# Exponentials left unscaled and the scale put on the result, in two attentions, and a heads stage that begins with keys and values

## The chip, the cores and the metric

One core of a Trainium2 chip runs the whole program in one launch. The metric is device microseconds (us) from start to end. A core has five engines, each with an instruction stream of its own: PE (matrix multiplies; a matmul's stationary operand is loaded by a weight load, shown as PEld), DVE (vector), ACT (scalar functions), POOL (GpSimd) and SP, which here only issues DMAs. They wait for each other through semaphores. PSUM has 8 banks of 128 x 512 fp32; PE writes them, DVE and ACT empty them.

## The reference

The program is one inference step of a small encoder trunk for two groups of frames: 1024 new frames of one stream (the prompt, 8 tiles of 128 rows) and 64 frames of another that has 512 cached ones (the sample, a ninth tile of 64 rows). In transposed form there are T = 1088 columns, cut into chunks of 384, 384 and 320.

The even layer has two head groups from one input projection (an mLSTM, and a latent attention, MLA, 8 heads of 64 with a low-rank latent for keys and values and one for queries), one output projection over both, and a feed-forward. The odd layer has a chunk-band attention (16 heads of 64, a window of about 640 keys with a bias) and a feed-forward. Cut to the part that the change touches:

```
cq = rmsnorm(h @ W_dq, g_q)            # query latent, 384 wide
q_nope, q_rope = cq @ W_uq ...         # per head 64 + 32
k_nope, v      = ckv @ W_uk, ckv @ W_uv
p = softmax(scale * q.k + mask)        # MLA, causal by chunk of 64 frames
o = p @ v                              # o: (frames, 64) per head
x = x + concat(o_mlstm, o_mla) @ W_out
...
p = softmax(q.k + bias)                # band attention
o = p @ v
x = x + concat(o) @ W_o
```

## The kernel before

Most matmuls take fp32 data split in two parts, high and low (names in hi and lo), and make three passes (hi.hi, lo.hi, hi.lo) at the fast rate; ACT rounds the high part, DVE or POOL subtracts for the low one. Transposes and the product of probabilities with V stay plain fp32, in which one matmul shows as two records. The stages run one after the other, with a barrier between: load, mix0 (input projection and mLSTM), heads (queries, keys and values per head, from the latents, parked in HBM), mix0b (MLA attention and output projection), a feed-forward, mix (band attention with all its projections), a feed-forward and the final norm.

**Heads.** Items are one PSUM bank each: 8 tiles of weights for queries by 3 chunks (L1403), 4 tiles of key weights by 4 spans of 400 keys, then 13 tiles for values. Three results wait ahead of it: the norm of the query latent cqT, made at the end of mix0 (matmuls with ones L528, DVE L849 and L852, ACT root L775, DVE product L857), its high part (ACT L1415) and its low part (DVE L1447).

**mix0b.** Heads go in pairs; a pair has 18 steps, 9 query tiles for head e = 0 in the order S (sample), 0 to 7, and 9 for e = 1 in the order S, 7 to 0: 72 steps g in all. PE's order in a step is written by hand:

- turn(g), transposes of the probabilities p (L1672), which wait for DVE's `normal`;
- score(g+1), the scores into pS (L1662);
- fillers, 2 or 3 groups of the output projection (L1637 to L1639), each into one of three banks F in rotation;
- weigh(g) (L1691), after ACT has copied the transposed p out as pT (keep, L1744 to L1748) and after the step before has emptied pO.

ACT's order is keep(g), exp(g+1) (L1734, which also sums each row), splits, and high(g) (L1754), the high part of pO. DVE's is maximum(g+1) (L1801), one emptied filler bank (L1794), normalise(g+1) (reciprocal L1809, then p times it, L1811), the other fillers, and low(g) (L1817). p has a single buffer. The output projection of a pair's own heads begins when all 18 steps have been split. SP loads queries, keys, values and weights by the step; `splits` is a table of the steps in which a unit of output weights is loaded.

**mix.** The same shape for 8 pairs of heads, 144 steps, tiles in the order 0 to 3, S, 4 to 7 for both e: turn L2194, score L2183, fillers from a list by step (projections for the next pair L2129 to L2131, output projection of the pair before L2141 to L2143, transposes L2151 and L2161), weigh L2212. DVE: L2393 adds the bias and takes the minimum, L2403 and L2405 normalise, L2364 adds the output groups to xT, L2413 is low. ACT: keep L2282, exp L2272, high L2293. In the last three steps of pairs 1 to 6 there are 6, 6 and 6 output groups, behind a block of transposes in the last, with three banks F for them. The first pair has no output groups beside it; the last has one or two in most steps and none of the projections.

## Time and profile before

| what | value |
|---|---|
| time, median of 3 runs | 3272.31 us (3272.21 to 3276.55) |
| the profiled execution | 3272.54 us, of which 3270.5 are the span |
| PE, share of the span | 93%, weight loads 90% |
| DVE, ACT, POOL | 38%, 31%, 26% |
| heads | 417 to 502 us |
| mix0b | 502 to 864 us |
| mix (band attention) | 1680 to 2427 us |

Read it so: PE works nearly all the time, so a change can gain only where PE waits, or by fewer or cheaper matmuls. In mix0b PE is busy for 300 of 362 us, in mix for 697 of 747, so there is some waiting in both, and there is more at the seams of the stages.

### The profile page before, as it was taken

The page shows a single profiled execution, that of the slowest core. Times are in us where ns is not written, and L with a number is a line of the kernel's source. Part 1 is how long each engine was busy: PE and PEld are TensorE (multiplying, and loading weights), DVE is VectorE, ACT ScalarE, POOL GpSimd, SP SyncE. Part 2 cuts the span into 40 slices and gives each one's busy share as a digit, 9 for nine tenths or more (in the row PEclk, how much of TensorE's full clock was granted, in tenths as well). Part 3 has the DMA queues.
Part 4 walks back from the last instruction along what each step waited for, and adds up shares of the span by engine and source line. Part 5 has one row for each costly group of instructions (what it writes and reads, how often), then busy time and mean ns, then how long its engine had stood idle before and what let it go on. Part 6 is the DMA issues. An engine that isn't in the chain of part 4 may idle for free. (4 is left out here: it accounts for less than half of the span.)

```text
span 3270.5 us, 46685 instructions
## 1 busy us (share of the span) xinstructions
PE 3056.0 (93%) x18884; PEld 2956.9 (90%) x18884; DVE 1257.3 (38%) x2672; ACT 1015.3 (31%) x1772; POOL 862.5 (26%) x437
## 2 busy tenths in 40 slices
PE   6999986888899999999989999999879999999998
PEld 5889976778799999999979899999859999999997
DVE  4423335666622222222243556666653222222223
ACT  4322234444421112121134544444443111121211
POOL 3211122211332223222233322323324222232220
PEclk8999988899999999999999999999999999999999
DMA  3133133111211111111021111111111111112101
GB/s 114 56 73 65 42 143 102 47 44 34 65 52 39 38 38 40 63 38 51 0 69 43 44 37 43 39 41 44 34 48 56 52 38 38 38 38 64 38 13 61
DMA packets 153853, 165.72 MB, mean 51 GB/s; under 512 B 9063, under 2 KB 137015, under 8 KB 153535
## 3 DMA queue, kind: packets, MB, share of 16 engines
q1 hardware_dynamic: 153726, 163.96, 16.4%
q8 instruction: 89, 1.46, 0.2%
q14 instruction: 38, 0.30, 0.0%
HBM read 140.78 MB, written 28.92 MB: 52 GB/s over the span
## 5 line engine op out<-in xcount | busy, mean ns | idle before, releaser
L236 PE MATMUL ffn_banks<-hhi,ffn_whi 128*128 128x384 f32 (+1 forms) x2112 | 693.0, 328 | 19.5 <-POOL hlo L217 13.2
L237 PE MATMUL ffn_banks<-hlo,ffn_whi 128*128 128x384 f32 (+1 forms) x2112 | 692.5, 328 | 0.0
L238 PE MATMUL ffn_banks<-hhi,ffn_wlo 128*128 128x384 f32 (+1 forms) x2112 | 692.3, 328 | 0.0
L1211 DVE TENSOR_TENSOR ffn_act<-ffn_silu,ffn_banks 128x384 f32<-128x384 f32 x132 | 70.2, 532 | 962.3 <-PE ffn_banks L238 945.7
L236 PEld LDWEIGHTS ffn_banks<-hhi,ffn_whi 128*128 128x128 f32 x2112 | 399.5, 189 | 21.0 <-issue 21.0
L1145 POOL TENSOR_TENSOR ffn_wlo<-ffn_stage,ffn_whi 128x2048 fp32r<-128x2048 f32 x66 | 303.3, 4609 | 423.7 <-ACT ffn_whi L1105 423.7
L237 PEld LDWEIGHTS ffn_banks<-hlo,ffn_whi 128*128 128x128 f32 x2112 | 399.3, 189 | 0.0
L238 PEld LDWEIGHTS ffn_banks<-hhi,ffn_wlo 128*128 128x128 f32 x2112 | 399.2, 189 | 0.0
L1217 DVE TENSOR_TENSOR xT<-xT,ffn_banks 128x384 f32<-128x384 f32 (+1 forms) x528 | 281.0, 532 | 240.4 <-PE ffn_banks L238 240.4
L238 PE MATMUL ffn_banks<-ffn_ahi,ffn_wlo 128*128 128x384 f32 (+1 forms) x1056 | 344.7, 326 | 0.0
L237 PE MATMUL ffn_banks<-ffn_alo,ffn_whi 128*128 128x384 f32 (+1 forms) x1056 | 344.6, 326 | 0.0
L236 PE MATMUL ffn_banks<-ffn_ahi,ffn_whi 128*128 128x384 f32 (+1 forms) x1056 | 344.6, 326 | 0.0
L1152 POOL TENSOR_TENSOR ffn_alo<-ffn_act,ffn_ahi 128x384 fp32r<-128x384 f32 x132 | 128.0, 970 | 792.7 <-ACT ffn_ahi L1117 792.7
L1113 ACT ACTIVATE ffn_silu<-ffn_banks 128x384 f32<-128x384 f32 x132 | 62.4, 474 | 620.5 <-PE ffn_banks L238 620.5
L1105 ACT ACTIVATE ffn_whi<-ffn_stage 128x2048 fp32r<-128x2048 f32 x66 | 124.1, 1909 | 363.6 <-PE ffn_banks L238 358.5
L2129 PE MATMUL mix_F<-hhi,mix_whi 128*128 128x384 f32 (+1 forms) x576 | 194.1, 337 | 7.9 <-POOL hlo L217 7.6
L238 PEld LDWEIGHTS ffn_banks<-ffn_ahi,ffn_wlo 128*128 128x128 f32 x1056 | 198.3, 188 | 0.0
L236 PEld LDWEIGHTS ffn_banks<-ffn_ahi,ffn_whi 128*128 128x128 f32 x1056 | 198.3, 188 | 0.0
L237 PEld LDWEIGHTS ffn_banks<-ffn_alo,ffn_whi 128*128 128x128 f32 x1056 | 198.3, 188 | 0.0
L2131 PE MATMUL mix_F<-hhi,mix_wlo 128*128 128x384 f32 (+1 forms) x576 | 189.7, 329 | 0.0
L2130 PE MATMUL mix_F<-hlo,mix_whi 128*128 128x384 f32 (+1 forms) x576 | 189.4, 329 | 0.0
L482 PE MATMUL mix_F<-hhi,mix_whi 128*128 128x384 f32 (+1 forms) x528 | 180.0, 341 | 7.7 <-POOL hlo L217 7.6
(323 smaller groups left out, 5580.9 us busy)
## 6 DMA issues: line engine op xcount, KB each, us to landing
ffn_stage<-in_w_gate SPq DMA_DIRECT2D x22, 1024.0 KB
ffn_stage<-in_w_up SPq DMA_DIRECT2D x22, 1024.0 KB, 5.3
ffn_stage<-in_w_down SPq DMA_DIRECT2D x22, 1024.0 KB, 4.9
mix_wst<-in_w_qkv SPq DMA_DIRECT2D x24, 512.0 KB
mix_wst<-in_w_in SPq DMA_DIRECT2D x22, 512.0 KB
load_xin<-in_x_prompt SPq DMA_DIRECT2D x8, 512.0 KB, 4.6
mix0b_wst<-in_w_out SPq DMA_DIRECT2D x8, 512.0 KB
mix_wst<-in_w_out SPq DMA_DIRECT2D x8, 512.0 KB
```

What stands on the lines that cost most here:

```text
L236: nc.tensor.matmul(out, whi[:, k, :], hhi[:, k, c0:c0 + w], start=(k == 0), stop=False)
L237: nc.tensor.matmul(out, whi[:, k, :], hlo[:, k, c0:c0 + w], start=False, stop=False)
L238: last = nc.tensor.matmul(out, wlo[:, k, :], hhi[:, k, c0:c0 + w], start=False, stop=(k == kts - 1))
L482: nc.tensor.matmul(dst, wh, hhi[:, k, c0:c0 + w], start=(k == 0), stop=False)
L1105: nc.scalar.activation(whi[m][:], stage[m][:], ACT.Copy).then_inc(w_hi[m], 1)
L1145: nc.gpsimd.tensor_tensor(wlo[m][:], stage[m][:], whi[m][:], ALU.subtract).then_inc(w_lo[m], 1)
L1152: nc.gpsimd.tensor_tensor(alo[:, f, c0:c0 + w], act32[:, f, 0:w], ahi[:, f, c0:c0 + w], ALU.subtract).then_inc(a_lo, 1)
L1211: nc.vector.tensor_tensor(act32[:, f, 0:w], silu[:, f, 0:w], banks[:, 2 * f + 1, 0:w], ALU.mult).then_inc(product, 1)
L1217: nc.vector.tensor_tensor(x, x, banks[:, 4 + k % 4, 0:w], ALU.add).then_inc(added, 1)
L2129: nc.tensor.matmul(dst[:, 0:w], wh, hhi[:, k, c0:c0 + w], start=(k == 0), stop=False)
L2130: nc.tensor.matmul(dst[:, 0:w], wh, hlo[:, k, c0:c0 + w], start=False, stop=False)
L2131: last = nc.tensor.matmul(dst[:, 0:w], wl, hhi[:, k, c0:c0 + w], start=False, stop=(k == KT - 1))
```

## The change

1. **Scale moved behind the product.** In both attentions p is no longer multiplied by the reciprocal of its row sum. turn(g) waits for the exponentials alone. Since the scale belongs to a query row, the product is turned round: weigh now loads pT as the stationary operand and moves the 64 columns of V of its own head, so pO is query rows by 64. DVE's evict(g) multiplies pO by the reciprocal into a new buffer otok (query rows by the pair's 128 columns).
2. **Flips.** The output projection wants the result transposed and split. High and low per step (two operations for each of 216 steps) go; in their place stands one flip for each pair and tile (36 in mix0b, 72 in mix): a PE transpose of otok into a bank of F, ACT's high part from the bank, DVE's low part, which frees the bank. A flip is the first item of work in each of the pair's steps 10 to 17 and in the next pair's step 0. ACT takes it after exp(g+1); DVE, which empties banks in order, takes it before the step's other banks.
3. **DVE order.** maximum or minimum (g+1), reciprocal(g), all the banks of step g, evict(g).
4. **mix0b's start and SP.** Keys are loaded and split ahead of the queries, the first low part of the keys is DVE's rather than POOL's, the rotary parts have semaphores of their own, and in each step the load of output weights comes ahead of those of queries and keys.
5. **Heads.** The norm of the query latent moves from mix0's end into heads. Items are now 4 key tiles (a matmul of the norm behind each of the first three), 13 value tiles, and the query tiles last. The norm and its splits are placed among the value items. The latent of keys and values is split in 4 spans. Values have 6 output slots, each bank a semaphore pair.

```diff
@@ both attentions: turn, weigh, DVE @@
-                pe.wait_ge(s["normal"], g + 1)
+                pe.wait_ge(s["exped"], g + 1)
...
                 if g:
-                    pe.wait_ge(s["lo"], g)
+                    pe.wait_ge(s["evicted"], g)
                 for b, (_, kw, vt) in enumerate(tiles):
-                    last = nc.tensor.matmul(pO[:, 0:w], V[0:kw, vt, :], pT[0:kw, b * P:b * P + w],
+                    last = nc.tensor.matmul(pO[0:w, 0:H], pT[0:kw, b * P:b * P + w], V[0:kw, vt, own(e)],
                                             start=(b == 0), stop=(b == len(tiles) - 1))
...
-                v.tensor_scalar(p_[0:w, 0:width], p_[0:w, 0:width], inv[0:w, col], None, ALU.mult).then_inc(s["normal"], 1)
+            def evict(g):
...
+                dve.wait_ge(s["summed"], g + 1)
+                v.tensor_scalar(otok[0:w, t, own(e)], pO[0:w, 0:H], inv[0:w, g % 4:g % 4 + 1], None, ALU.mult)\
+                 .then_inc(s["evicted"], 1)
@@ mix0b: the order of work @@
+    def flips(g):
+        if g == 0:
+            return []
+        pair, n = divmod(g - 1, STEPS)
+        return [("flip", pair, ORDER[1][n - N])] if n >= N else []
+
+    def work(g):
+        return flips(g) + fillers(g)
...
+                if x[0] == "flip":
+                    _, pair, t = x
+                    w = tile_width(t)
+                    pe.wait_ge(s["evicted"], STEPS * pair + N + ORDER[1].index(t) + 1)
+                    if n >= FB:
+                        pe.wait_ge(emptied[n % FB], n // FB)
+                    nc.tensor.transpose(F[:, n % FB, 0:w], otok[0:w, t, :], S["ident"][0:w, 0:w]).then_inc(filled[n % FB], 1)
+                    return
...
                 keep(g)
                 if g + 1 < PAIRS * STEPS:
                     exp(g + 1)
+                for x in flips(g):
+                    high(x)
...
-                high(g)
...
             for g in range(PAIRS * STEPS):
                 pair, n = divmod(g, STEPS)
                 h, i = divmod(g, N)
+                if g in splits:
+                    load_w(splits[g])
                 if i == 2 and h + 2 < B_HEADS:
                     load_q(h + 2)
                 if i == 4 and h + 2 < B_HEADS:
                     load_k(h + 2)
-                if g in splits:
-                    load_w(splits[g])
@@ mix: the list of work by step @@
+        if s > N:
+            x.append(("flip", p, TILES[s - N - 1]))
+        if s == 0 and p:
+            x.append(("flip", p - 1, TILES[-1]))
@@ mix, DVE @@
             for g in range(PAIRS * STEPS):
-                work = fillers(g // STEPS, g % STEPS)
-                early = 0 if any(x[0] == "proj" for x in work) else len(work) // 2
                 if g + 1 < PAIRS * STEPS:
                     minimum(g + 1)
-                for x in work[:early]:
+                reciprocal(g)
+                for x in fillers(g // STEPS, g % STEPS):
                     empty(x)
-                if g + 1 < PAIRS * STEPS:
-                    normalise(g + 1)
-                for x in work[early:]:
-                    empty(x)
-                low(g)
+                evict(g)
@@ end of mix0 @@
-            for c in range(NC):
-                mean_of("cq_mean", c, cq_var, Q_RANK)
-            normalise(cqT, RQ, G_Q, cq_var, 2)
@@ heads @@
+    for i in range(4):
+        items += [("k", i, n) for n in range(len(spans))]
+        if i < NC:
+            items.append(("cq", i))
+    items += [("v", n) for n in range(VN)]
...
+                    if n == 2:
+                        dve.wait_ge(s["rooted"], 1)
+                        for k in range(RQ):
+                            dve.scalar_tensor_tensor(out=cqT[:, k, :], in0=cqT[:, k, :], scalar=S["gains"][:, G_Q + k:G_Q + k + 1],
+                                                     in1=var[:], op0=ALU.mult, op1=ALU.mult).then_inc(s["normed"], 1)
+                    if n == 8:
+                        dve.wait_ge(s["q_hi"], 1)
+                        dve.tensor_tensor(q_lo, cqT[:], q_hi, ALU.subtract).then_inc(s["q_lo"], 1)
```

First, DVE in mix (mix_pS are the scores, mix_F the ring of banks, mix_pO the product of the attention): one of a pair's last steps, with six output groups. Before:

```order
L2393 ISA mix_p,mix_least<-mix_pS,mix_nb 128x640
L2393 ISA mix_least 128x1
L2364 TENSOR_TENSOR xT<-xT,mix_F 128x384 x3
L2403 RECIPROCAL mix_inv<-mix_total 128x1
L2405 TENSOR_SCALAR mix_p<-mix_p,mix_inv 128x640
L2364 TENSOR_TENSOR xT<-xT,mix_F 128x384 x3
L2413 TENSOR_TENSOR mix_o_lo<-mix_pO,mix_o_hi 64x128
```

And now, the same step:

```order
L2525 ISA mix_p,mix_least<-mix_pS,mix_nb 128x640
L2525 ISA mix_least 128x1
L2535 RECIPROCAL mix_inv<-mix_total 128x1
L2473 TENSOR_TENSOR mix_o_lo<-mix_F,mix_o_hi 128x128
L2496 TENSOR_TENSOR xT<-xT,mix_F 128x384 x6
L2542 TENSOR_SCALAR mix_otok<-mix_pO,mix_inv 128x64
```

The product over 640 columns is gone, and the low part (L2473), which waits for ACT, now stands ahead of all six banks instead of behind them.

Second, PE in the same stage, from the scores of one step to its weigh. Before:

```order
L2183 MATMUL mix_pS<-mix_kk,mix_qb 128x384
L2141 MATMUL mix_F<-mix_o_hi,mix_whi 128x384
L2142 MATMUL mix_F<-mix_o_lo,mix_whi 128x384
L2143 MATMUL mix_F<-mix_o_hi,mix_wlo 128x384
L2141 MATMUL mix_F<-mix_o_hi,mix_whi 128x384
...
L2212 MATMUL mix_pO<-mix_pT,mix_V 128x128 x5
```

And now:

```order
L2310 MATMUL mix_pS<-mix_kk,mix_qb 128x384
L2270 MATMUL mix_F<-ident,mix_otok 128x128
L2263 MATMUL mix_F<-mix_o_hi,mix_whi 128x384
L2264 MATMUL mix_F<-mix_o_lo,mix_whi 128x384
L2265 MATMUL mix_F<-mix_o_hi,mix_wlo 128x384
...
L2339 MATMUL mix_pO<-mix_V,mix_pT 128x64 x5
```

One transpose (L2270) has come in ahead of the output groups and takes one of the three banks of F; weigh has as many matmuls as before, with 64 moving columns.

Third, SP in mix0b, about step 12, where mix0b_wst is the buffer of output weights, mix0b_q_in and mix0b_k_in those of queries and keys. Before:

```order
L1583 DMA mix0b_V<-park_heads_v 128x4x128
L1585 DMA mix0b_V<-park_heads_v 64x128
L1562 DMA mix0b_q_in<-park_heads_q 64x1088
L1564 DMA mix0b_q_in<-park_heads_q 32x1088
L1557 DMA mix0b_wst<-in_w_out 128x1024
L1569 DMA mix0b_k_in<-park_heads_k 64x1600
```

And now:

```order
L1686 DMA mix0b_V<-park_heads_v 128x4x128
L1688 DMA mix0b_V<-park_heads_v 64x128
L1660 DMA mix0b_wst<-in_w_out 128x1024
L1665 DMA mix0b_q_in<-park_heads_q 64x1088
L1667 DMA mix0b_q_in<-park_heads_q 32x1088
L1672 DMA mix0b_k_in<-park_heads_k 64x1600
```

The load of the weights has moved past the two loads of queries, which wait for their buffer.

## Rows read from the trace of the kernel before

**Rows 1.** The page's line of engines: busy us, share, instructions.

```profile
PE 3056.0 (93%) x18884; PEld 2956.9 (90%) x18884; DVE 1257.3 (38%) x2672; ACT 1015.3 (31%) x1772; POOL 862.5 (26%) x437
```

**Rows 2.** Timeline, end of mix0 and start of heads.

```profile
402.91 3.71 PE L528 MATMUL mix_F<-mix_raw,ones 128*128 128x384 f32 x12
...
411.89 3.88 DVE L857 SCALAR_TENSOR_TENSOR latents_cqT<-latents_cqT,gains,mix_kw 128x1088 f32<-128x1088 f32 x3 [1.18 <-ACT mix_kw L775]
...
416.87 2.92 ACT L1415 ACTIVATE hhi<-latents_cqT 128x3264 fp32r<-128x3264 f32 x1 [5.01 <-PEq L64]
...
419.82 3.56 DVE L1447 TENSOR_TENSOR hlo<-latents_cqT,hhi 128x3264 fp32r<-128x3264 f32 x1 [4.05 <-ACT hhi L1415]
...
424.38 0.66 PE L1403 MATMUL heads_bank<-hhi,heads_w_hi 128*128 128x384 f32 x1 [17.76 <-POOL heads_w_lo L1437]
```

**Rows 3.** Tile heads_w_in: users, min, median and max ns, and DMA landing.

```profile
L1413 ACT ACTIVATE heads_w_hi<-heads_w_in x12: 409/517/526, 419.7 to 471.7; 128x384 fp32r<-128x384 f32 x8, 128x256 fp32r<-128x256 f32 x4
L1437 POOL TENSOR_TENSOR heads_w_lo<-heads_w_in,heads_w_hi x12: 740/1010/4250, 420.3 to 472.2; 128x384 fp32r<-128x384 f32 x8, 128x256 fp32r<-128x256 f32 x4
DMA to landing us min/median/max: 2.4/2.7/3.1
```

**Rows 4.** Timeline, end of heads: the last park, and mix0b's first DMA.

```profile
499.77 0.32 SPq L1377 DMA_DIRECT2D park_heads_v<-heads_out  x1
502.68 0.48 SPq L1562 DMA_DIRECT2D mix0b_q_in<-park_heads_q  x1
```

**Rows 5.** Stretches of time in mix0; the granted clock follows POOL's column.

```profile
205.50:211.30 5.80, 0.15 (x1) 0.16 (x2) 5.56 (x4) 2.32 (x4) 3.04 (x1) 0.66 0.40 116
211.30:216.00 4.70, 4.70 (x19) 4.25 (x20) 1.69 (x3) 0.34 (x2) 0.00 (x0) 0.50 0.12 33
```

**Rows 6.** Groups by shape, PE in mix0b: busy, mean ns, idle before and releaser.

```profile
L1691 PE MATMUL mix0b_pO<-mix0b_pT,mix0b_V 128*128 128x128 f32 x576 | 77.8, 282 | 12.8 <-ACT mix0b_pT L1744 10.8 <-DVE hlo L1817 2.0
L1672 PE MATMUL mix0b_pP<-ident,mix0b_p 128*128 128x128 f32 x288 | 46.5, 290 | 28.1 <-DVE mix0b_p L1811 27.1
L1672 PE MATMUL mix0b_pP<-ident,mix0b_p 64*128 64x64 f32 x32 | 3.9, 246 | 4.8 <-DVE mix0b_p L1811 4.8
```

**Rows 7.** Timeline of mix0b: weighs at 564, 587 and 594 us.

```profile
564.27 1.36 PE L1691 MATMUL mix0b_pO<-mix0b_pT,mix0b_V 128*128 128x64 f32 x10
...
585.12 1.06 ACT L1715 ACTIVATE mix0b_whi<-mix0b_wst 128x1024 fp32r<-128x1024 f32 x1 [8.44 <-DMA mix0b_wst<-in_w_out]
...
587.36 2.93 PE L1691 MATMUL mix0b_pO<-mix0b_pT,mix0b_V 128*128 128x128 f32 x12 [6.63 <-ACT mix0b_pT L1744]
...
593.91 1.28 PE L1691 MATMUL mix0b_pO<-mix0b_pT,mix0b_V 128*128 128x128 f32 x10
...
594.47 0.49 DVE L1811 TENSOR_SCALAR mix0b_p<-mix0b_p,mix0b_inv 128x512 f32<-128x512 f32 x1
...
595.02 0.66 PE L1672 MATMUL mix0b_pP<-ident,mix0b_p 128*128 128x128 f32 x4
```

**Rows 8.** Groups by shape, PE in the whole of mix, columns as in rows 6.

```profile
L2194 PE MATMUL mix_pP<-ident,mix_p 128*128 128x128 f32 x480 | 76.3, 279 | 28.3 <-DVE mix_p L2405 28.3
```

**Rows 9.** The same for pairs 1 to 6, then for the last pair.

```profile
L2194 PE MATMUL mix_pP<-ident,mix_p 128*128 128x128 f32 x365 | 57.5, 278 | 11.5 <-DVE mix_p L2405 11.5
L2194 PE MATMUL mix_pP<-ident,mix_p 128*128 128x128 f32 x60 | 9.9, 285 | 13.8 <-DVE mix_p L2405 13.8
```

**Rows 10.** Timeline of one of a pair's last steps in mix.

```profile
2156.32 0.34 PE L2141 MATMUL mix_F<-mix_o_hi,mix_whi 128*128 128x384 f32 x1
...
2156.52 0.82 DVE L2393 CUSTOM_DVE_ANT_0 mix_p<-mix_pS,mix_nb 128x640 f32<-128x640 f32 x1 [0.53 <-PE mix_pS L2183]
...
2157.27 1.48 DVE L2364 TENSOR_TENSOR xT<-xT,mix_F 128x384 f32<-128x384 f32 x3
2157.36 0.33 PE L2141 MATMUL mix_F<-mix_o_hi,mix_whi 128*128 128x384 f32 x1
2157.39 0.83 ACT L2272 ACTIVATE mix_p<-mix_p,mix_least 128x640 f32<-128x640 f32 x1 [0.75 <-DVE mix_least L2393]
```

More of the change, by code:

```diff
@@ L520, in mean @@
                 return last
-            def cq_mean(x):
-                c = x[1]
-                c0, w = CHUNKS[c]
-                dst = begin(x)[:, 0:w]
-                pe.wait_ge(s["sq"], NC + RQ - 1 + c + 1)
-                for k in range(RQ):
-                    last = nc.tensor.matmul(dst, S["ones"][:], raw[:, k, c0:c0 + w], start=(k == 0), stop=(k == RQ - 1))
-                return last
             def cached(x):
@@ L1375, in _ @@
[L1375 to L1379 removed]
+            for i in range(4):
+                load(i + 2)
+                park_k(i)
+                if i == NC - 1:
+                    await_filled(sp, ("cq", NC - 1))
+                    sp.dma_start(rope[:], D["rope_q"]).then_inc(s["rope_in"], 16)
@@ L1416, in _, with square @@
+            def square(c):
+                c0, w = CHUNKS[c]
+                if c:
+                    await_filled(act, ("cq", c - 1))
+                act.activation(sq[:, :, 0:w], cqT[:, :, c0:c0 + w], ACT.Square).then_inc(s["sq"], 1)
+            high(0)
             split_w(0)
+            for n in range(1, len(spans)):
+                high(n)
+            square(0)
             split_w(1)
-            act.activation(kv_hi[:], ckvT[:], ACT.Copy).then_inc(s["hi"], 1)
-            act.wait_ge(s["v_loaded"], 16)
@@ L1432, in _ @@
         @block.gpsimd
         def _(pool):
-            for i in range(len(tiles)):
-                kts = RQ if tiles[i][2] == "q" else RK
+            for i, (name, _) in enumerate(tiles):
+                kts = RK if name == "w_uk" else RQ
                 pool.wait_ge(s["w_hi"], i + 1)
@@ L1475, in mix0b_stage @@
+                    dve.tensor_tensor(dst, dst, turned[:, c0:c0 + w], ALU.add).then_inc(emptied[number[x] % FB], 1)
 def mix0b_stage(nc, S, D):
@@ L1498, in mix0b_stage @@
     FB = 3
-    number = {x: n for n, x in enumerate(groups)}
+    def flips(g):
[5 more added lines that the diff above has]
+        return flips(g) + fillers(g)
+    END = PAIRS * STEPS
+    program = [x for g in range(END) for x in work(g)] + flips(END) + behind
+    number = {x: n for n, x in enumerate(program)}
+    flip_no = {x: n for n, x in enumerate(x for x in program if x[0] == "flip")}
     def begun(g):
@@ L1700, in _ @@
                     score(g + 1)
-                for x in fillers(g):
+                for x in work(g):
                     fill(x)
                 weigh(g)
-            for x in behind:
+            for x in flips(END) + behind:
                 fill(x)
@@ L1778, in _ @@
                     split_w(splits[g])
-                high(g)
+            for x in flips(END):
+                high(x)
         @block.vector
@@ L1845, in _ @@
                     split_q(h + 1)
-                low(g)
-            for x in behind:
+                evict(g)
+            for x in flips(END) + behind:
                 empty(x)
@@ L1947, in mix1_stage @@
     ahead += [("kc", 0, 0), ("vtok", 0, 0)]
-    behind = [("out", PAIRS - 1, j, c) for j, c in outs]
+    behind = [("flip", PAIRS - 1, TILES[-1])] + [("out", PAIRS - 1, j, c) for j, c in outs]
     def key_of(x):
@@ L2143, in fill @@
                     last = nc.tensor.matmul(dst[:, 0:w], wl, oh, start=False, stop=True)
+                elif kind == "flip":
+                    _, pair, t = x
+                    w = tile_width(t)
+                    pe.wait_ge(s["evicted"], STEPS * pair + N + TILES.index(t) + 1)
+                    last = nc.tensor.transpose(dst[:, 0:w], otok[0:w, t, :], S["ident"][0:w, 0:w])
                 elif kind == "vtok":
@@ L2258, in take @@
                     nc.scalar.activation(kk[own(e), e, T:KEYS], bank(x)[own(e), :], ACT.Copy).then_inc(s["kc_hi"], 1)
+                elif x[0] == "flip":
+                    _, pair, t = x
+                    w = tile_width(t)
+                    await_filled(act, x)
+                    nc.scalar.activation(o_hi[:, pair % 2, t * P:t * P + w], bank(x)[:, 0:w], ACT.Copy).then_inc(s["hi"], 1)
                 elif x[0] == "ktok":
@@ L2333, in _ @@
                     split_w(unit_no[weights_at(pair, n)])
-                high(g)
+            take(behind[0])
         @block.vector
```

429 lines of the change are left out of this document (248 added, 181 removed).

## The prediction

> **What bounds the kernel now.** I read the page's line of engines first: PE is busy for 93% of the span [rows 1], so only PE's waits, or fewer or cheaper matmuls, can pay. Next came the groups by shape in the two attention stages, for what ended PE's waits. In mix0b the transposes of p waited 28.1 and 4.8 us for DVE's product with the reciprocal, and weigh waited 12.8 us [rows 6]; in mix the transposes waited 28.3 us for the same product [rows 8]. Last I read the timelines at the places where these waits are long, and at the seam before heads, where PE stands for 17.76 us [rows 2]. A wait is worth its length only if nothing else is late behind it, so each is followed to what is late next.
>
> **Heads: -11.2 us.** Before, the last chunk of the query latent's norm begins on PE at 402.91, the product L857 ends at 415.77, a barrier follows to 416.85, ACT's high part takes 2.92 and DVE's low part 3.56, and the first matmul starts at 424.38 [rows 2]. Now none of it stands ahead of the first item. mix0's own PE work ends without the norm matmuls: they were last from 402.9 on, and a first group of six (1.9 us, half of the 3.71 for twelve) stood further ahead, so it ends at about 401. I add 0.7 for the last evictions, 1.1 for the barrier (from 415.77 to 416.85), 2.7 for the load of the weights, 0.4 and 0.74 for their high and low parts (smallest values of [rows 3]): PE starts at 406.6, 17.8 us earlier. The norm's matmuls come into heads: 1.9 + 3.7 = 5.6 us [rows 2]. The clock gives nothing back: after 5.8 us of idle PE the granted clock was still 0.50 for the next 4.7 us in mix0 [rows 5], as it is after a long wait, and the new pause is as long (401 to 406.6).
>
> What is late next is the low part of the query latent. DVE cannot empty value banks until the last key park has landed, by my estimate 5 us into the values (a load of 128 KB took 2.7 [rows 3], and the last park, with the barrier, 2.9 [rows 4]; a key park is several times as large). Then it has nine copies of .65 (.49 for 384 columns [rows 10], scaled to 512), 3.88 for the norm and 3.56 for the low part [rows 2]: 5 + 5.9 + 3.9 + 3.6 = 18.4 us. PE has 13 value items of six matmuls of .23 (.173 for 384 columns [rows 10]): 18.0. With the handovers that is a stall of about 1 us. Sum: -17.8 + 5.6 + 1 = -11.2. Bounds: -15 (no stall, and the pause short enough that the clock stays up for a part) and -3 (DVE's chain 8 us late, since DVE and POOL pass each other badly here: POOL's part of the weights took 4.25 us in its longest case, with DVE at work beside it, against 1.01 [rows 3]).
>
> The start of mix0b has the keys ahead of the queries, but the first exponential waits on ACT behind the split of the first block of mLSTM output, the last DMA of the opening, so I give only the product's 1.1 us, which is counted below.
>
> **mix0b, turn: -27.9.** Between the row sum and the transposes stood a reciprocal of .16 and a product of .49 for 512 columns; from the product's start to the transposes .55 went by, some .75 with the reciprocal [rows 7]. The waits were 32.9 us in some 40 steps, .8 each on average, so nearly all of each goes. I leave 5.0 for the widest tiles and the first step.
>
> **mix0b, weigh: -10.8.** Two waits of ACT for the output weights: 8.44 us before the split at 585.12, which holds back keep, and so weigh by 6.63 at 587.36 [rows 7]; a second like it makes up the 10.8 of [rows 6]. That DMA was queued on SP behind loads that wait for a buffer. The new order issues it ahead of them. Nothing is late behind it that has not 5 us to spare. Bounds: -12.8 and, should the weights be late for another reason, 0.
>
> **Flips, cost on PE: +12.** 36 + 72 transposes; 288 transposes took 46.5 us of overlapping busy time, and the four at 595.02 followed at .11 each [rows 7], so .11 each: 4 and 8 us.
>
> **Flips, stalls.** This is the term I trust least. In a step, let f be the start of the first item behind the scores. DVE starts the minimum at f + .20, takes .82 for 640 columns, ACT starts exp .87 after the minimum and takes .83, and each hands on [rows 10]. Only then come ACT's high part and DVE's low part, some .3 each for 128 columns by my estimate from DVE's .49 for 384. With .05 to .1 between operations and .2 up to the minimum the flip's bank is free at f + .88 + M + X, with M and X the lengths of minimum and exp: f + 2.53 at 640 columns. The ring has three banks, and PE wants this one again for the third item behind the flip, at f + .11 + 1.04 (two output groups are 1.04, from 2156.32 to 2157.36 [rows 10]). Stall: 1.38 us. DVE then empties a bank each .49 (three in 1.48 [rows 10]), as fast as PE fills them, so it does not grow. In mix pairs 1 to 6 have it at steps 15 and 16 in full, 1.15 at step 17 and 1.07 at the next step 0 (narrower tiles), and .15 each at steps 11, 13 and 14, where a projection of 24 matmuls stands between: 5.4 us. In mix0b only every third step has three groups and reaches that far. Scaled from the 640 columns, it is 1.6 for the tile of 768, .9 for that of 384, and 1.5 at the pair's end: 4.0 for each of 4 pairs, 16 us.
>
> **mix: +11.6 before weigh.** Pairs 1 to 6 had waits of 11.5 us at the transposes, 1.9 each [rows 9]. Each now pays 5.4 of stalls and 1.0 of flips against 1.9, and .2 at the banks: +4.3, times 6 is +25.8. The last pair has one or two groups in a step, so that the flip's bank is not wanted again in the same step, and had 13.8 us of waits [rows 9]. Each loses .8 or so, as in mix0b, but the flip's 1 us comes on top and some wait for exp stays: -10.7. The first pair has no output groups; the rest of the 28.3 [rows 8], 3.0, and its short waits at weigh give -3.5. The sum is +11.6, with bounds of -4 (stalls half as long) and +38 (the full stall in all seven steps: 6 x 4.3 more).
>
> **weigh turned round: -6.** The moving side halves, from 128 columns to 64. The trace has both: ten records of 128 x 128 from 593.91 to the transposes at 595.02 are .111 each, and ten of 128 x 64 took 1.36 with their modelled end, no less than the 1.28 of the former [rows 7]. So the pitch does not go by the moving columns, and I take nothing per record. What may be gained is half a pitch, .055, at the first record of each of 216 weighs, which has no record of its own kind before it: 12 us. The bounds are 0 and -12, and no row is nearer to one; I take -6.
>
> The Trainium skill (TensorE: Matmul & The Clock Gate, section LDWEIGHTS) has a weight load take its columns divided by 1.2 in ns, whatever its rows, which is 107 ns for 128 columns. For 128 columns the trace agrees, with .111. By that rule weigh gains nothing in the 192 prompt steps, but where pT gives 64 columns of weights, in the 24 sample steps of ten records, half of each: 24 x 10 x .055 = 13 us more, an estimate; no row here shows such a load in a stream.
>
> **The sum.** Heads -11.2; mix0b -27.9 - 10.8 + 4 + 16 = -18.7; mix +11.6; weigh -6: -24.3. From the profiled execution's 3272.5, which is the median of the runs to .2, this gives 3248.
>
> **Rivals.**
> - *The gains of heads or of the output weights come late (smaller gain).* DVE's chain is 8 us late in heads, or the waits at the transposes give way to waits for exp in half of the cases (+12). For: DVE's chain and PE's values are within 1 us of each other. Time 3248 + 8 = 3256 to 3260, or 3268 with both. Chance .2.
> - *The stalls take all (slower).* ACT takes the flip behind an exp that itself waits for DVE. If no projection hides it, the full stall falls on all 54 steps with three items behind the flip (7 in pairs 1 to 6 of mix, 3 in the 4 pairs of mix0b), and if another bank's copy comes before it on ACT it is .5 longer (a row of 384 columns takes .49 on DVE [rows 10]): 54 x 1.9 = 103 us where I have 16 + 6 x 5.4 = 48. Then the time is 3248 + 55 = 3303. It decides at 24 us over my 48, that is at 1.34 per step of the 54. Against: the projections. Chance .12, of which .05 ends within .2%.
> - *Stalls half as long.* If the stall takes up waits that PE would have had in the same step, -24: 3224. Chance .1.
> - *weigh goes by moving columns.* The 576 records [rows 6] and the 960 that mix has by its key tiles fall from .111 to .056: 1536 x .055 = 84 us, 3164. The Trainium skill (TensorE: Matmul & The Clock Gate, Back-to-back issue gap) has an isolated matmul's spacing go by N/2.4 + 2.5 ns, which would halve with N. The ten records of 128 x 64 speak against it. Chance .03.
> - *As forecast*, 3238 to 3258: chance .55.
>
> **Numbers.** A measurement here can tell some .2% (6.5 us) from no change. Faster by more than that: .55 + .1 + .03 + .15 of the first rival = .83; within it .05 + .05 = .10; slower .07. The range for 8 in 10 reaches to the smaller gain on one side and most of the way to the shorter stalls on the other: 3226 to 3264.
>
> **What would show it.** Heads' first matmul 17 to 18 us earlier, and no wait over 2 us behind the values. No wait of weigh over 2 us at steps 12 and 32. Waits at the transposes of mix0b under 8 us in all. In mix, output groups that wait 1.2 to 1.5 us for DVE's low part in steps 15 and 16 of each pair. weigh's 128 x 64 records .11 apart. The prediction is wrong if ACT or DVE, not the ring, holds PE in more steps than these, or if heads gives back what its start gains.

## The result

The changed kernel took 3222.64 us (median of 4 runs, 3221.55 to 3225.16) beside 3273.51 for the kernel before on the same chip: the ratio is .9842, 95% interval .9828 to .9857. It is faster by some 51 us, where I had forecast 24 and a range that ended at 3226. The direction was right, the size was off by a factor of two, and the time lies just outside the range.

The profiled execution has a span of 3223.4 us. The page's line of engines answers to [rows 1]:

```profile
PE 3048.7 (95%) x18992; PEld 2941.0 (91%) x18992; DVE 1134.7 (35%) x2568; ACT 976.0 (30%) x1665; POOL 853.0 (26%) x436
```

PE's busy time is only 7 us less than before. By this line some 40 of the 47 us between the two spans are waiting.

**Where it came from, by stage.** The clearest measure of an attention stage is the first and the last start of its transposes of p, as the view by tile gives them (min, median and max ns, then the two starts). Before:

```profile
L1672 PE MATMUL mix0b_pP<-ident,mix0b_p x328: 216/273/474, 519.4 to 846.3; 128*128 128x128 f32 x144, 64*128 64x64 f32 x16, 64*64 64x64 f32 x4
L2194 PE MATMUL mix_pP<-ident,mix_p x560: 216/273/475, 1747.7 to 2408.7; 128*128 128x128 f32 x161, 64*128 64x64 f32 x21, 64*64 64x64 f32 x5
```

And after:

```profile
L1785 PE MATMUL mix0b_pP<-ident,mix0b_p x328: 216/273/473, 504.7 to 795.9; 128*128 128x128 f32 x144, 64*128 64x64 f32 x16, 64*64 64x64 f32 x4
L2321 PE MATMUL mix_pP<-ident,mix_p x560: 216/273/477, 1702.8 to 2360.7; 128*128 128x128 f32 x161, 64*128 64x64 f32 x21, 64*64 64x64 f32 x5
```

mix0b went from 326.9 to 291.2 us (-35.7), mix from 661.0 to 657.9 (-3.1). All ahead of mix0b's first transpose is 14.7 shorter. My terms for the same stretches were -18.7 and +11.6, with another -6 for weigh in both together, and -11.2 for heads. Each stage did better than I said, mix0b by most. The three add up to 53.5 us where the spans differ by 47.1: between the two attentions the changed kernel's trace is 5.5 us longer (1.7 of it before the feed-forward's first matmul, where the last flips stand), and .9 behind mix.

**The seam before heads**, by the timeline of the changed kernel:

```profile
399.96 0.87 ACT L1440 ACTIVATE heads_kv_hi<-latents_ckvT 128x800 fp32r<-128x800 f32 x1 [1.08 <-PEq L64]
402.24 0.42 ACT L1436 ACTIVATE heads_w_hi<-heads_w_in 128x256 fp32r<-128x256 f32 x1 [1.41 <-DMA heads_w_in<-in_w_uk]
402.74 0.73 POOL L1494 TENSOR_TENSOR heads_w_lo<-heads_w_in,heads_w_hi 128x256 fp32r<-128x256 f32 x1 [29.73 <-ACT heads_w_hi L1436]
403.52 0.70 PE L1426 MATMUL heads_bank<-heads_kv_hi,heads_w_hi 128*128 128x400 f32 x1 [5.11 <-POOL heads_w_lo L1494]
404.02 0.54 PE L1426 MATMUL heads_bank<-heads_kv_lo,heads_w_hi 128*128 128x400 f32 x1
```

It runs as worked out: a wait of 5.11 us where 17.76 stood [rows 2]. After it a matmul takes .54, and the granted clock is .50 for the next 4.5 us, the low level; in the kernel before it is .50 for 4.8 us behind the wait. No wait shows behind the values.

**The attentions**, groups by shape of PE, mix0b first, then mix (columns as in [rows 6]):

```profile
L1804 PE MATMUL mix0b_pO<-mix0b_V,mix0b_pT 128*128 128x64 f32 x576 | 72.0, 270 | 2.7 <-ACT mix0b_pT L1855 2.7
L1748 PE MATMUL mix0b_F<-hhi,mix0b_whi 128*128 128x384 f32 x128 | 48.4, 378 | 7.8 <-DVE hlo L1909 7.0 <-issue 0.7
L1785 PE MATMUL mix0b_pP<-ident,mix0b_p 128*128 128x128 f32 x288 | 44.9, 284 | 3.9 <-ACT mix0b_p L1845 3.6
...
L1748 PE MATMUL mix0b_F<-hhi,mix0b_whi 128*128 128x320 f32 x64 | 22.3, 349 | 3.8 <-DVE hlo L1909 3.8
```

```profile
L2321 PE MATMUL mix_pP<-ident,mix_p 128*128 128x128 f32 x480 | 76.1, 279 | 4.1 <-ACT mix_p L2404 3.9
...
L2263 PE MATMUL mix_F<-mix_o_hi,mix_whi 128*128 128x384 f32 x128 | 47.2, 369 | 16.8 <-DVE mix_o_lo L2473 15.3 <-ACT mix_ktok L2394 1.3 <-DVE xT L2496 0.2
```

The waits at the transposes, 28.1 [rows 6] and 28.3 us [rows 8], are down to 3.9 and 4.1, and weigh's 12.8 in mix0b to 2.7. In their place PE waits before output groups for DVE's low part of a flip: 10.8 us in mix0b, 15.3 in this row of mix and 20.5 in all of mix's stretch.

### The profile page after: what moved, and what is told of

Its sections match the earlier page's. It is cut to its first block and busy times, and to the rows that moved or that the text cites. A ratio compares the mean times of both kernels' runs of the same rounds, so it can differ in the third digit from the quotient of the medians.

```text
span 3223.4 us, 46994 instructions
## 1 busy us (share of the span) xinstructions
PE 3048.7 (95%) x18992; PEld 2941.0 (91%) x18992; DVE 1134.7 (35%) x2568; ACT 976.0 (30%) x1665; POOL 853.0 (26%) x436
## 5 line engine op out<-in xcount | busy, mean ns | idle before, releaser
L236 PEld LDWEIGHTS ffn_banks<-hhi,ffn_whi 128*128 128x128 f32 x2112 | 399.4, 189 | 20.9 <-issue 20.9
L2251 PE MATMUL mix_F<-hhi,mix_whi 128*128 128x384 f32 (+1 forms) x576 | 196.0, 340 | 10.9 <-POOL hlo L217 7.7
```

Of the source, the lines that this page charges most:

```text
L236: nc.tensor.matmul(out, whi[:, k, :], hhi[:, k, c0:c0 + w], start=(k == 0), stop=False)
L2251: nc.tensor.matmul(dst[:, 0:w], wh, hhi[:, k, c0:c0 + w], start=(k == 0), stop=False)
```

## The experiments

Times below are medians; a ratio is to the kernel before, run beside it on the same chip, with its 95% interval. The intervals are about .0015 wide to each side, which is 5 us, so for small terms I read the stretch between the first and the last transpose as well, from one profiled execution each. Traces of the same code show how far to trust it: mix's stretch is 661.0, 660.9, 661.1 and 660.9 us in four kernels with the band attention of before and 657.9 and 658.1 in two with the new one, so a difference of 1 us counts; mix0b's is 326.9 and 330.7, and 291.2 and 292.7, so there less than some 4 us says little. Ahead of heads two traces of the same code lie up to 7.5 us apart (its first matmul at 424.4 and at 416.9 us).

**1. weigh as before.**

```diff
-                    last = nc.tensor.matmul(pO[0:w, 0:H], pT[0:kw, b * P:b * P + w], V[0:kw, vt, own(e)],
+                    last = nc.tensor.matmul(pO[:, 0:w], V[0:kw, vt, :], pT[0:kw, b * P:b * P + w],
```

> The changed kernel with weigh as it was before: V's 128 columns are the stationary operand and the transposed exponentials move, in both attentions. The result lands transposed, so the numbers that are evicted are not the attention's; all else is as in the changed kernel. Theory A (most of what I missed lies in weigh: the two traces have 32 us less issue time for it, 13 of them in the 24 sample steps whose stationary operand is now 64 columns wide, the rest at the first record of each prompt step): 3223 + 32 = about 3255. Rival B (the saving is the 6 us that I forecast, and the rest of the miss comes from stalls that are shorter): about 3229.

3236.31 us (3228.28 to 3238.98), ratio .9890 (.9873 to .9906): 14 us more than the changed kernel. The stretch in mix is 666.7 us (+8.8), that in mix0b 291.0 (-.2); the execution that they come from was the fastest of the four. Both theories were off: 32 was too much, 6 too little.

**2. Prompt steps move 128 columns.** The same line, with `V[0:kw, vt, :]` and `pO[0:w, 0:P]` where a tile has 128 rows.

> The changed kernel, but in the 192 prompt steps weigh moves all 128 columns of V instead of the head's 64 (the extra 64 columns of the result are not used); the 24 sample steps stay at 64 stationary and 64 moving columns. Theory A: the prompt steps save about .09 us each through the shorter first and last records, so 3223 + 17 = about 3240. Rival B (prompt steps gain nothing from fewer moving columns; the gain is all in the sample steps): 3223.

3225.71 us (3224.63 to 3229.21), ratio .9857 (.9841 to .9874). The stretches are 661.9 us in mix (+4.0) and 292.6 in mix0b (+1.4). By the intervals between starts weigh's records take .05 us more in a prompt step, not .09. Of that, 4.0 us in mix's 128 prompt steps, .03 each, arrives as time: theory A's sign, at a third of its size.

**3. The sample steps as before.** The line of experiment 1, in the steps with 64 rows alone.

> The changed kernel, but in the 24 sample steps weigh is as before: V's 128 columns stationary, 64 columns of transposed exponentials moving (what is evicted there is not the attention's result). The prompt steps stay turned. Theory A (the stationary operand's columns set the pitch, and in the traces a sample step's weigh went from 1.296 to .870 us): 24 x .43 = 10 us, 3223 + 10 = 3233. Rival B (the sample steps hide it behind waits on ACT and DVE): 3223 to 3226.

3222.12 us (3218.63 to 3223.89), ratio .9855 (.9841 to .9870): nothing that the runs can tell from the changed kernel's .9842. The stretches are +3.3 us in mix and +2.8 in mix0b, of which mix0b's lies within what that stretch moves by itself. So the pitch does follow the 64 stationary columns. In mix the records grow by 16 x .43 = 6.9 us and the stretch by 3.3, so about half arrives as time, between the two theories. That waits take up the rest is likely, but no run shows it.

The row for such steps in mix in the changed kernel, then the one of the kernel of experiment 1:

```profile
L2339 PE MATMUL mix_pO<-mix_V,mix_pT 128*64 128x64 f32 x128 | 10.9, 228 | 0.0
```

```profile
L2339 PE MATMUL mix_pO<-mix_pT,mix_V 128*128 128x64 f32 x128 | 16.0, 268 | 0.0
```

These are eight records in each of mix's 16 sample steps. Their busy time falls from 1.0 to .68 us a step (16.0 and 10.9 over 16), with no wait ahead of either.

**4. SP's order as before, on the changed kernel.**

```diff
-                if g in splits:
-                    load_w(splits[g])
                 if i == 2 and h + 2 < B_HEADS:
                     load_q(h + 2)
                 if i == 4 and h + 2 < B_HEADS:
                     load_k(h + 2)
+                if g in splits:
+                    load_w(splits[g])
```

> The changed kernel with SP's loads of output weights in mix0b behind the loads of queries and keys of the same step, as before. Theory A (SP's queue held the weights back, and with them ACT, keep and weigh): 3223 + 10 = 3233. Rival B (with the product gone the loads no longer come late, since queries and keys are split earlier): 3223.

3240.22 us (3239.18 to 3243.14), ratio .9901 (.9885 to .9918): 17.6 more, and +18.0 in mix0b's stretch. The order is worth more than its waits: in mix0b's stretch PE waits 10.5 us more, and the time between waits grows by 7.5. The timeline has one of them:

```profile
654.69 1.06 ACT L1826 ACTIVATE mix0b_whi<-mix0b_wst 128x1024 fp32r<-128x1024 f32 x1 [7.15 <-DMA mix0b_wst<-in_w_out]
...
656.99 0.29 DVE L1909 TENSOR_TENSOR hlo<-mix0b_F,hhi 128x128 fp32r<-128x128 f32 x1 [7.24 <-ACT hhi L1865]
...
657.34 0.69 PE L1748 MATMUL mix0b_F<-hhi,mix0b_whi 128*128 128x384 f32 x1 [6.92 <-DVE hlo L1909]
657.82 0.53 PE L1749 MATMUL mix0b_F<-hlo,mix0b_whi 128*128 128x384 f32 x1
```

A late load of weights holds ACT, ACT holds the flip, and the flip holds the ring. After 6.92 us of waiting a matmul takes .53 instead of .34. The stretches of the same trace (the granted clock stands behind POOL's column):

```profile
657.30:662.00 4.70, 4.67 (x20) 4.67 (x21) 2.11 (x6) 0.49 (x1) 0.87 (x1) 0.50 0.00 0
662.00:667.00 5.00, 5.00 (x27) 5.00 (x27) 2.23 (x9) 1.74 (x7) 0.00 (x0) 0.66 0.00 0
```

**5. SP's new order, on the kernel before.** The same edit the other way round.

> The kernel before with only SP's loads of output weights in mix0b put ahead of the loads of queries and keys of the same step. Theory A (the two waits of weigh, 10.8 us, go, and with them the low clock behind each, some 2.7 + 1.7 us of issue time by the rows at 587 to 593 and 685 to 690 us; in the changed kernel putting the loads back cost 17.6): the kernel before minus 14 to 17. Rival B (my forecast: the waits alone): minus 10.8.

3258.41 us (3253.07 to 3266.22), ratio .9970 (.9960 to .9981): -9.8 us, with an interval from -6 to -13, and -7.1 in mix0b's stretch. That is rival B's number; theory A's -14 lies outside the interval. In the stretch the waits are 8.5 us less and the time between them 1.4 more, and the mean granted clock is .96 in both kernels: the low stretches behind the two waits went, and others came elsewhere. Taken alone the new order gives what I forecast. In the changed kernel it keeps away 18: there the late loads also hold the flips, whose waits are 6.6 of the 10.5 us.

**6. The product back on the exponentials, behind the first bank.**

```diff
+                v.tensor_scalar(p_[0:w, 0:width_of(t)], p_[0:w, 0:width_of(t)], inv[0:w, col], None, ALU.mult).then_inc(s["normal"], 1)
...
-                pe.wait_ge(s["exped"], g + 1)
+                pe.wait_ge(s["normal"], g + 1)
```

> The changed kernel with the product on the exponentials back on DVE, in the place that it had (behind the first bank emptied), and the eviction without a scale; turned weigh and flips stay. Theory A (the product stood on the chain from row sum to transposes, and its removal took the waits at the transposes from 62.8 to 14.6 us): 3223 + 45 to 50, about 3270. Rival B (part of these waits would be taken up by the stalls behind the flips, which come in the same steps): 3223 + 30, about 3253.

3341.37 us (3339.81 to 3346.57), ratio 1.0212 (1.0195 to 1.0230): 119 more, +47.4 in mix0b's stretch and +71.7 in mix's. Neither theory came near. The timeline shows what the product does in a step with a flip:

```profile
2006.63 0.29 DVE L2479 TENSOR_TENSOR mix_o_lo<-mix_F,mix_o_hi 128x128 fp32r<-128x128 f32 x1 [1.15 <-ACT mix_o_hi L2396]
...
2007.69 2.36 POOL L2590 TENSOR_TENSOR mix_wlo<-mix_wst,mix_whi 128x1024 fp32r<-128x1024 f32 x1 [9.21 <-ACT mix_whi L2371]
...
2007.96 2.44 DVE L2543 TENSOR_SCALAR mix_p<-mix_p,mix_inv 128x640 f32<-128x640 f32 x1
```

It now comes after the flip and beside POOL's work, and takes 2.44 us where the group's usual length is .55. In mix 26 of the 144 products take over 1 us, 54 us together, and each of them overlaps an operation of POOL.

The kernel before has such meetings too, which I had not seen: 13 products over 1 us in mix, 32 us together, all beside POOL. This is one:

```profile
1876.36 5.17 POOL L2460 TENSOR_TENSOR mix_qb<-mix_raw,mix_qa 64x1088 fp32r<-64x1088 f32 x2
1876.36 2.78 DVE L2405 TENSOR_SCALAR mix_p<-mix_p,mix_inv 128x512 f32<-128x512 f32 x1
...
1879.20 0.55 PE L2194 MATMUL mix_pP<-ident,mix_p 128*128 128x128 f32 x3 [1.02 <-DVE mix_p L2405]
```

Of the 11.5 us of waits at the transposes in [rows 9] for pairs 1 to 6, 9.0 follow such a meeting: about 1.0 us at step 12 of each pair and .4 to .5 at step 2. The other two waits stand where the first pair gives way to the second. In all other steps of these pairs the product stands in the same chain, between row sum and transposes, and PE does not wait.

**7. The product ahead of the flip.** As experiment 6, but straight behind the row sum.

> The changed kernel with the product on the exponentials back on DVE, right behind the row sum and ahead of the flip's low part and, in steps with a flip, ahead of every bank. With the product behind the flip it was 3341. Theory A (what the product costs is its place on the chain from row sum to transposes; behind the flip it stood behind ACT's high part too): the waits at the transposes come back at about 48 us and the ring's stalls grow by .7 each in some 24 steps: 3223 + 65 = 3288. Rival B (the product in itself costs that much once the ring carries flips): 3330 to 3341.

3325.03 us (3320.40 to 3329.58), ratio 1.0175 (1.0159 to 1.0191): 102 more (by the ratio, which allows for the chip, 109), where theory A said 65; it is rival B's number. The stretches are +51.5 in mix0b and +51.3 in mix. Of these 103 us only 71 are waits; 31 are longer records between them, and the mean granted clock goes from .98 to .94 in mix0b and from 1.00 to .98 in mix. Only 7 products in mix take over 1 us here (18 us together), against 26 in experiment 6, and it is in mix that experiment 6 is the slower. In mix the three rows that hold the waits are

```profile
L2258 PE MATMUL mix_F<-hhi,mix_whi 128*128 128x384 f32 x357 | 126.9, 355 | 21.2 <-DVE mix_o_lo L2480 21.0 <-issue 0.2
...
L2328 PE MATMUL mix_pP<-ident,mix_p 128*128 128x128 f32 x480 | 78.4, 285 | 17.9 <-DVE mix_p L2544 17.5
...
L2270 PE MATMUL mix_F<-mix_o_hi,mix_whi 128*128 128x384 f32 x128 | 48.6, 379 | 24.9 <-DVE mix_o_lo L2480 24.1
```

The waits at the transposes come back in part, 17.9, but the ring pays more, 45 us in these two shapes against 18 in the changed kernel. Flips in the ring are only cheap with the product gone: the two parts of the change carry each other.

**8. Flips last in their step.**

```diff
-        return flips(g) + fillers(g)
+        return fillers(g) + flips(g)
```

and the same in mix's list of work.

> The changed kernel with each flip as the last item of its step instead of the first, in both attentions. ACT takes it after the exponentials as before, DVE after the step's other banks. Theory A (PE waits 32 us in all for a ring bank that DVE cannot free, since the flip's low part stands ahead of the banks and waits for ACT behind its exp; as the last item the flip is filled when exp is done): 3223 - 28, about 3195. Rival B (the flip then holds its bank into the next step and delays weigh's eviction and that step's banks as much): 3215 to 3225.

3204.63 us (3197.03 to 3211.18), ratio .9792 (.9767 to .9818): 16 to 18 less than the changed kernel. That is halfway between the theories. mix0b's stretch is 275.8 us (-15.4), somewhat more than the waits that theory A counts there; mix's is 652.4, only -5.5. The waits for the flips' low part are gone in both (10.8 to 0 in mix0b, 20.5 to 0 in mix), but in mix a wait of 2.00 us stands once in each of pairs 1 to 6:

```profile
1834.15 2.54 DVE L2513 TENSOR_SCALAR mix_nb<-mix_b_in 128x256 f32<-128x256 f32 x1
1834.17 2.37 POOL L2574 TENSOR_TENSOR mix_wlo<-mix_wst,mix_whi 128x1024 fp32r<-128x1024 f32 x1 [2.86 <-ACT mix_whi L2366]
...
1837.79 0.43 PE L2264 MATMUL mix_F<-mix_o_hi,mix_whi 128*128 128x320 f32 x1 [2.00 <-DVE mix_V L2505]
1838.04 0.45 PE L2265 MATMUL mix_F<-mix_o_lo,mix_whi 128*128 128x320 f32 x1
```

DVE's bias and POOL's low part of the weights start within .02 us of each other, and DVE's takes 2.54 us. Behind this wait the granted clock is .53 for 3.6 us. The same operation took .34 in a step where POOL was done (experiment 7's trace).

**9. ACT takes the splits ahead of the flips as well.** In ACT's step the two loops change places.

> The kernel with each flip last in its step, and ACT takes a flip behind the splits of its step instead of ahead of them. In the kernel with flips last alone a new wait of 2.00 us stood in mix once in each of pairs 1 to 6: ACT's split of weights waited for the flip, POOL's low part of the weights then ran beside DVE's shifted bias, and that took 2.54 us. Theory A (the collision is the cause, and the clock falls after the wait): the 12 us of waits go and some issue time with them, 3204 - 12 to 16, about 3190. Rival B (the output group waits for its bank in any case, since the flips hold one): 3204.

3180.17 us (3176.63 to 3183.16), ratio .9727 (.9714 to .9741). mix's stretch is 632.9 us, 19.5 less than with the flips last alone, more than theory A's 12 to 16. PE's waits in mix fall by 9.5 us and the time between them by 10.1. The bias still meets POOL, but 1.7 us later in POOL's operation:

```profile
1831.16 2.36 POOL L2578 TENSOR_TENSOR mix_wlo<-mix_wst,mix_whi 128x1024 fp32r<-128x1024 f32 x1 [3.04 <-ACT mix_whi L2366]
...
1832.85 0.83 DVE L2517 TENSOR_SCALAR mix_nb<-mix_b_in 128x256 f32<-128x256 f32 x1
```

It takes .83 us in place of 2.54, and the six waits of 2.00 are down to .28 each. The length of this meeting was the cause of the waits; rival B is out.

**10. Weights loaded five steps earlier**, on top of 9: `if g + 5 in splits: load_w(splits[g + 5])`.

> Flips last and splits first as in the run above, and in mix0b SP issues each load of output weights five steps earlier, so that it stands behind no load of queries. The changed kernel still had one wait of weigh of 2.68 us for these weights, with the granted clock at .58 for the next 4.1 us. Theory A: 2.7 us of wait and about 1.7 of clock go: 4 less than the run above. Rival B (the loads are not late by their place in the queue but by their own time): no less.

3174.44 us (3165.95 to 3178.96), ratio .9701 (.9683 to .9720). mix0b's stretch is 273.1 against 278.0 us: -4.9 where theory A said 4, and the one wait of weigh, 2.61 us, is gone. As a whole the gain is less sure: the ratios' intervals overlap a little, and the two profiled executions differ by only .5 us, since the second is 5 us longer between the attentions and in mix. This is the fastest version by its median, 3.0% under the kernel before and 1.4% under the change as it was made.

**11. Heads alone, and mix of before.** The first has both attentions of the kernel before, the second the changed kernel with mix of before.

> The kernel before with only the heads part of the change (the norm of the query latent in heads, keys and values first); both attentions as before. Theory A (heads is worth what the trace shows between the end of mix0 and mix0b's first DMA, 15.4 us): 3273 - 15.4 = 3258. Rival B (a part of it is only the shift of mix0b's own opening): 3262 or more.

> The changed kernel with the band attention of before. Theory A (in mix the flips and their stalls give back nearly all of what the transposes' waits and weigh gave: -42 of waits and issue, +39): 3223 + 3 = 3226. Rival B (mix lost, as I forecast, some 8 us): 3215.

Heads alone: 3260.21 us (3259.59 to 3263.77), ratio .9958 (.9943 to .9972), or -14 us with 5 to each side: nearer theory A, though rival B's 3262 is still within the interval. With mix of before: 3226.11 (3223.51 to 3228.26), ratio .9849 (.9826 to .9872), and its stretch is 660.9 us, +3.0. So the change in mix is worth 3 us, and what is left for mix0b is 51 - 14 - 3 = 34, near its stretch's 35.7.

## Why the prediction was half the size

In short: in mix0b the waits fell by what I had summed up, 23 us. What failed is the step from a wait to the time that it costs: I took each wait for its printed idle time, and the time between waits fell by 12.7 us too. With it, weigh's -6 was too small: 9 to 14 us by experiment 1.

**Heads: right.** -11.2 forecast, -14 measured, inside my bounds. The first matmul stands 5.11 us behind mix0's last; I had 5.6. In the traces it is 20.9 us earlier where I said 17 to 18, but these lie several us apart ahead of heads for the same code. The stall of 1 us behind the values did not come: no PE wait shows in heads behind the start. That and the norm's matmuls, which I put at 5.6 us and which take 4.6 of issue time, are the difference.

**mix0b, turn (-27.9): right as a list of idle times, too small as time.** The rows have 32.9 us before [rows 6] and 10.3 after, of which 6.39 is the opening (2.9 there before, with the scores later); so my sign "under 8 us in all" failed, by the opening. All of PE's waits in the stretch fell by 23.0 us, and my terms for them (-27.9 - 10.8 + 16) were -22.7. But the stretch fell by 35.7: the time between waits fell by 12.7 too, where I had +4 for the flips and some -2 for weigh. The step that failed is the one that took a printed wait for the whole of the time lost by it. The same step of the first pair, tile of 768 columns, shows it. The kernel before:

```profile
544.87 0.87 PE L1672 MATMUL mix0b_pP<-ident,mix0b_p 128*128 128x128 f32 x6
...
548.00 1.50 PE L1691 MATMUL mix0b_pO<-mix0b_pT,mix0b_V 128*128 128x128 f32 x12
...
549.50 0.69 DVE L1811 TENSOR_SCALAR mix0b_p<-mix0b_p,mix0b_inv 128x896 f32<-128x896 f32 x1
...
550.24 0.33 PE L1672 MATMUL mix0b_pP<-ident,mix0b_p 128*128 128x128 f32 x1 [0.75 <-DVE mix0b_p L1811]
```

The changed kernel:

```profile
526.32 0.82 PE L1785 MATMUL mix0b_pP<-ident,mix0b_p 128*128 128x128 f32 x6
...
529.39 1.45 PE L1804 MATMUL mix0b_pO<-mix0b_V,mix0b_pT 128*128 128x64 f32 x12
...
530.72 0.44 PE L1785 MATMUL mix0b_pP<-ident,mix0b_p 128*128 128x128 f32 x2
```

The step was 5.37 us and is 4.40, .97 less, with a printed wait of .75. Another .05 is weigh's shorter first record (1.50 and 1.45 for the twelve). The tail of the last record is .12: its end is modelled .27 behind its start and the idle time counts from there, but where nothing holds it the next one starts .16 behind it here, and .11 in most steps. The last .05 is the first transpose of the step, .16 and .11 to the next. So a wait that goes is worth its idle time and .1 to .2 more. The intervals from weigh's last record to the transposes, idle time taken off, add up to 18.5 us in mix0b and 24.0 in mix before, and to 11.6 and 20.0 now: 11 us. They stay at 11.5 and 20.7 with weigh as before (experiment 1), and rise to 17.1 and 21.8 with the product back (experiment 7).

**mix0b, weigh's waits (-10.8): the idle time right, what stood behind it missed.** Both long waits went; one of 2.68 us is left, at step 22. Behind each of the two the granted clock had been low:

```profile
587.30:592.80 5.50, 5.44 (x22) 5.15 (x23) 2.46 (x7) 3.29 (x6) 4.03 (x2) 0.50 0.01 3
...
684.80:690.00 5.20, 5.12 (x27) 4.88 (x27) 4.04 (x11) 2.03 (x7) 1.55 (x1) 0.67 0.01 3
```

At .50 for 5.5 us and .67 for 5.2 us, 2.7 + 1.7 = 4.4 us of work were given away. The row at 587.36, twelve records in 2.93 us, stood among my own [rows 7], and I read only its wait. Whether this time comes back with the wait stays open: experiment 4 has it (some 11 us of waits for 17.6 of time), experiment 5, on the kernel before, has not (-9.8 us in all for waits of 10.8). I do not count it as shown.

**weigh's turn (-6): too small, and so was my first account of it.** By the intervals between starts, weigh's records took 32 us less in the changed trace. With weigh as before they take 19 of these 32 again; the other 13 are the tails behind it, 11, and slower records. And not all of the 19 is time: experiment 1 gives back 14 by the runs (with 5 to each side) and 8.6 by the stretches, 8.8 of it in mix. By its records weigh's own is .05 a prompt step (10 us in 192) and .43 in each of the 24 sample steps (10 us), where the stationary operand went from 128 to 64 columns. This is the estimate that stood in the prediction as a sentence of its own, by the Trainium skill (TensorE: Matmul & The Clock Gate, section LDWEIGHTS): a weight load goes by its columns alone, so a load of 64 would take half as long, 13 us in all. The traces agree with the rule in its sign and roughly in its size (.43 us a step where the estimate has .55), but the time gained is under half of it (3.3 us in mix's 16 steps, where the estimate has 9). I left it out of the sum for want of a row.

**Flips on PE (+12) and their stalls: right in mechanism, and in time near my sum.** I had 16 us for mix0b; the rows have 10.8 and, for the flips' own waits, 2.8. In mix I had 32; PE waits 20.5 us there for the low parts and 1.8 for the flips' own, and beside these waits the scores' records take 4.5 us longer than before and the groups' 7.8, so that in time they are near the 32. A step of mix with six groups:

```profile
2111.82 0.27 PE L2270 MATMUL mix_F<-ident,mix_otok 128*128 128x128 f32 x1
...
2112.02 0.82 DVE L2525 CUSTOM_DVE_ANT_0 mix_p<-mix_pS,mix_nb 128x640 f32<-128x640 f32 x1 [0.78 <-PE mix_pS L2310]
2112.89 0.83 ACT L2404 ACTIVATE mix_p<-mix_p,mix_least 128x640 f32<-128x640 f32 x1 [0.75 <-DVE mix_least L2525]
2113.72 0.26 ACT L2390 ACTIVATE mix_o_hi<-mix_F 128x128 fp32r<-128x128 f32 x1
2114.00 0.29 DVE L2473 TENSOR_TENSOR mix_o_lo<-mix_F,mix_o_hi 128x128 fp32r<-128x128 f32 x1 [1.08 <-ACT mix_o_hi L2390]
2114.35 0.45 PE L2263 MATMUL mix_F<-mix_o_hi,mix_whi 128*128 128x384 f32 x1 [1.21 <-DVE mix_o_lo L2473]
```

The flip began at 2111.82 and its bank was free at 2114.3, 2.5 us later; I had 2.53, and a stall of 1.38 (1.21 and the tail of .16). Steps 15 and 16 of each pair are as forecast. Step 17 and the next step 0 paid .5 each, under half of my 1.15 and 1.07, and steps 11, 13 and 14 nothing. Experiment 8 takes these waits away and so shows that they are the ring's.

**mix, turn: the number right, the reason wrong.** I read the waits of pairs 1 to 6, 1.9 us each, as the product's place between row sum and transposes. Nine of the 11.5 us are its meetings with POOL (experiment 6), and they went with it all the same.

**Sum.** By the traces I had too little by 15 us in mix0b, 11 in mix and 3 to 4 in heads, and 6 of it was lost again outside the three: 23 us in the traces, 27 by the medians. Of the 26 in the attentions 11 are tails of waits that went, 3 to 8 weigh's own records over my 6 (by the stretches and by the runs of experiment 1), and the rest, 7 to 12, I cannot divide: slower records behind long waits, and an error of my single terms. The tails were read from the traces of several kernels; no run was made for them alone.

## What to carry to other kernels

A wait that goes gives back more than its printed idle time: the tail of the matmul ahead of it and, at times, the slow clock behind it (experiment 4, but not experiment 5); so read the durations of the records around a wait before you price it, and look at what ran beside the operation that ended it. If in-order engines share a ring, an item that needs a second engine belongs at the end of the step, where that engine's earlier work is done. And a part of a change must be tried within the changed kernel as well as alone: SP's order was worth 10 us on the old kernel and 18 on the new, and the product on p 102 to 119 us on the new, where all of its waits in the old were some 62 (no run took it from the old kernel alone).

## What the runs showed of the hardware

A DVE product or sum with a scalar, from SBUF to SBUF in fp32 with one input, does not run beside an operation of POOL: its record stretches to the end of POOL's and a little more. The bias of 128 x 256 took 2.54 us beside POOL's 2.37 and .34 without, the product of 128 x 640 took 2.44 beside 2.36 and .55 without. Wherever it began beside POOL's operation, with more than .1 us of that left, the bias ended .15 us behind POOL's end, and the product .22, .29 or .35 behind it for 384, 512 and 640 columns. In experiment 8's rows DVE's record starts .02 us ahead of POOL's, and still POOL's took its usual 2.37. The Trainium skill (SBUF — State Buffer, section Who interferes with whom) calls the pair of ports that the two share an exclusive lock, held for a whole instruction; the traces agree. It counts operations of a tensor with a scalar among those that can take the pair with one input, which both of these are. Experiment 9 shortened the meeting from 2.54 to .83 us by moving ACT's flip behind its splits, and mix's stretch fell by 19.5 us.
